# State-space part of a two-block kernel: the decay matrices as single-pass products in two parts, and the closing norm multiplication moved into the attention

## The reference, cut to what matters

```python
a_cum = jnp.cumsum(A, -1)
Lmat = jnp.exp(segsum(A))            # exp(a_cum[l] - a_cum[s]) where s <= l, else 0
y_diag = einsum('bclhn,bcshn,bhcls,bcshp->bclhp', Cc, Bc, Lmat, X)
chunk_states = einsum('bclhn,bhcl,bclhp->bchpn', Bc, exp(a_cum[..., -1:] - a_cum), X)
# carried over the chunks:  state = state * exp(a_cum[..., -1]) + chunk_states
y_off = einsum('bclhn,bchpn,bhcl->bclhp', Cc, prev, exp(a_cum))
y = (y_diag + y_off + d_skip * xs) * silu(z)
y = y * rsqrt(mean(y**2, -1) + eps) * norm_w
```

## Time and profile before

| what | us |
|---|---|
| median of 3 runs (lowest, highest) | 3704.17 (3702.64, 3704.63) |
| span of the profiled execution, first to last instruction | 3696.6 |
| difference of the two (what lies around the span) | 7.6 |
| first stage of the state space, first to last instruction | 308.7 to 319.7 |
| in it, end of VectorE's last instruction / of ScalarE's last | 318.6 / 319.7 |
| in it, end of VectorE's small chain (`adt`) / start of the product that needs it | 315.1 / 316.8 |
| in it, VectorE's first three instructions, together | 308.75 to 309.5 |
| second stage of the state space | 320.0 to 398.8 |
| in it, one square of ScalarE with its accumulator read | 0.9 |
| first products of the sparse attention | 399.1 |
| small tables issued with the key choice / first wait for them | 71.7 to 75.3 / 101.5 |

### The profile page before, as it was taken

How to read it: one execution, slowest core, us unless ns; L and a number is a source line. 1 busy time by engine, 2 the same in 40 slices (tenths; PEclk the granted TensorE clock), 3 DMA queues, 4 the chain that set the end, 5 groups by cost and what they waited for, 6 DMA issues and landing times. The chain is left out here.

```text
span 3696.6 us, 53818 instructions
## 1 busy us (share of the span) xinstructions
PE 3395.2 (92%) x18624; PEld 2593.7 (70%) x18624; DVE 2611.2 (71%) x4213; ACT 2064.5 (56%) x3299; POOL 374.7 (10%) x300
## 2 busy tenths in 40 slices
PE   8999989699969998998699999899989995999996
PEld 5444668577748764877588888788648784888885
DVE  3996755688762376663899999632766638999996
ACT  2663551488731475552477777523755524777674
POOL 0012000122121002000011111010020000111110
PEclk9999899799989999999899999999999997999998
DMA  3000011767261101013699999611010136999997
GB/s 147 23 1 3 2 69 70 295 257 270 100 230 42 46 10 44 2 60 141 233 396 379 384 390 379 253 43 46 2 52 1 54 117 240 388 380 394 380 381 285
DMA packets 115346, 645.96 MB, mean 175 GB/s; under 512 B 14048, under 2 KB 17120, under 8 KB 62944
## 3 DMA queue, kind: packets, MB, share of 16 engines
q1 hardware_dynamic: 94720, 569.15, 39.3%
q0 software_dynamic: 15984, 58.20, 5.3%
q10 hardware_dynamic: 4464, 16.25, 1.1%
HBM read 581.17 MB, written 62.39 MB: 174 GB/s over the span
## 5 line engine op out<-in xcount | busy, mean ns | idle before, releaser
L3375 DVE TENSOR_TENSOR low_ring<-mix,high_ring 128x2048 fp32r<-128x2048 f32 x256 | 576.7, 2284 | 41.4 <-ACT high_ring L3324 41.4
L3324 ACT ACTIVATE high_ring<-mix 128x2048 fp32r<-128x2048 f32 x256 | 477.0, 1931 | 80.3 <-PEq L141 80.3
L3263 PE MATMUL ps<-high_ring,x_high 128*128 128x512 f32 x1024 | 409.0, 399 | 8.5 <-DVE low_ring L3375 5.5
L3265 PE MATMUL ps<-high_ring,x_low 128*128 128x512 f32 x1024 | 399.6, 390 | 0.0
L3264 PE MATMUL ps<-low_ring,x_high 128*128 128x512 f32 x1024 | 399.2, 390 | 0.0
L3375 DVE TENSOR_TENSOR low_ring<-more_raw,high_ring 128x2048 fp32r<-128x2048 f32 x128 | 290.1, 2286 | 24.6 <-ACT high_ring L3324 24.6
L3324 ACT ACTIVATE high_ring<-more_raw 128x2048 fp32r<-128x2048 f32 x128 | 246.3, 1924 | 0.0
L3263 PEld LDWEIGHTS ps<-high_ring,x_high 128*128 128x128 f32 x1024 | 192.2, 188 | 71.3 <-DVE low_ring L3375 18.3
L3265 PEld LDWEIGHTS ps<-high_ring,x_low 128*128 128x128 f32 x1024 | 192.2, 188 | 41.6
L3264 PEld LDWEIGHTS ps<-low_ring,x_high 128*128 128x128 f32 x1024 | 192.5, 188 | 37.4
L3263 PE MATMUL ps<-high_ring,h_high 128*128 128x512 f32 x512 | 205.5, 401 | 0.0
(11 more groups left out here) (506 smaller groups left out, 8091.1 us busy)
## 6 DMA issues: line engine op xcount, KB each, us to landing
mix<-in_expert_units SPq DMA_DIRECT2D x256, 1024.0 KB, 7.6
more_raw<-in_expert_units SPq DMA_DIRECT2D x128, 1024.0 KB, 8.6
raw_experts<-in_expert_units SPq DMA_DIRECT2D x16, 3072.0 KB, 11.5
expert_out<-out ACTq DMA_DIRECT2D x31, 512.0 KB, 2.6
qk_body<-residual SPq DMA_DIRECT2D x16, 512.0 KB, 7.0
mix<-in_w_turned SPq DMA_DIRECT2D x16, 512.0 KB, 4.1
qk_tail<-in_w_out SPq DMA_DIRECT2D x8, 1024.0 KB, 8.2
mix<-residual SPq DMA_DIRECT2D x16, 512.0 KB, 3.3
```

Source lines behind the costliest of these rows:

```text
L3263: nc.tensor.matmul(ps[:, bank, :], left_high, high, start=first, stop=False)
L3265: return nc.tensor.matmul(ps[:, bank, :], left_low, high, start=False, stop=final)
L3324: nc.scalar.activation(w_high[:, n % RING, :], raw[n % RAW_UNITS], ACT.Copy).then_inc(high_ready, 1)
L3375: nc.vector.tensor_tensor(w_low[:, n % RING, :], raw[n % RAW_UNITS], w_high[:, n % RING, :].bitcast(F32), ALU.subtract).then_inc(low_ready, 1)
```

## The change

Spans. The running sums inside a chunk are now also made transposed, in one product in the first stage: `adt` (128 x 64) turned by `upto` gives 64 rows, one per chunk and head, of 128 running sums. VectorE splits them into a rounded part and a remainder (`cum_high`, `cum_low`). GpSimd makes rounded (fp32r) copies of the identity, of `hidden` (for 4 heads) and of a selector of chunks, `chunk_r` (64 x 8 x 128). At the start of the second stage VectorE and GpSimd each multiply one part with the selector of heads: `sums_high` and `sums_low` (64 x 1024 each). From then on the spans of a chunk are, per bank, three single-pass fp32r products: identity x hidden, chunk selector x sums_high, chunk selector x sums_low. `a_upto` and VectorE's product per chunk are gone. `hidden` is loaded as one 128 x 128 tile, with a new table `places`, among the small tables of `choose_keys`; the 256 KB load in the first state-space stage is gone.

Norm. The eight products with `root` and `norm_w` leave the state space and stand on VectorE in the attention, one in each of its iterations p = 4 to 11. The reciprocal stays.

```diff
@@ attend_pairs: VectorE, loop over p
                 copy_groups(p)
+                if gated and 4 <= p < 4 + T:
+                    rows, root, weight = gated
+                    nc.vector.scalar_tensor_tensor(out=rows[:, p - 4, :], in0=rows[:, p - 4, :],
+                                                   scalar=root[:, p - 4:p - 3], in1=weight, op0=ALU.mult,
+                                                   op1=ALU.mult)
                 if p >= 3:
                     write(p - 3)
@@ state_space, first stage
+                pe.wait_ge(read, 12)
+                nc.tensor.matmul(ps[0:TH, 5, 0:P], adt[:, :, :].rearrange("p t h -> p (t h)"), upto[:, :],
+                                 start=True, stop=True, skip_group_check=True).then_inc(turned_full, 1)
+            @block.gpsimd
+            def _(pool):
+                nc.gpsimd.tensor_copy(ident_r[:, :], ident[:, :])
+                nc.gpsimd.tensor_copy(hidden_r[:, :, :], hidden[:, :].unsqueeze(1).broadcast_to([P, 4, P]))
+                nc.gpsimd.tensor_copy(chunk_r[:, :, :], spread(places[0:TH, H:H + T], [TH, T, P]))
...
+                dve.wait_ge(turned_full, 1)
+                chain.step(nc.vector.tensor_copy(cum_high[:, :], ps[0:TH, 5, 0:P]))
+                nc.vector.tensor_tensor(cum_low[:, :], ps[0:TH, 5, 0:P], cum_high[:, :].bitcast(F32),
+                                        ALU.subtract)
@@ state_space, second stage, TensorE
                 def span(c):
-                    pe.wait_ge(a_upto_ready, c + 1)
-
+                    if c == 0:
+                        pe.wait_ge(sums_ready, 2)
+
+                    if c >= 1:
+                        pe.wait_ge(spans_ready, c)
                     for h in range(2):
-                        nc.tensor.matmul(ps[:, h, :], ident[:, :], hidden[:, :, :].rearrange("p a b -> p (a b)"),
+                        four = slice(4 * h, 4 * h + 4)
+                        nc.tensor.matmul(ps[:, h, :], ident_r[:, :], hidden_r[:, :, :].rearrange("p a b -> p (a b)"),
                                          start=True, stop=False)
-                        last = nc.tensor.matmul(ps[:, h, :], ones[:, :],
-                                                a_upto[:, 4 * h:4 * h + 4, :].rearrange("p a b -> p (a b)"),
+                        nc.tensor.matmul(ps[:, h, :], chunk_r[:, c, :],
+                                         sums_high[:, four, :].rearrange("p a b -> p (a b)"), start=False, stop=False)
+                        last = nc.tensor.matmul(ps[:, h, :], chunk_r[:, c, :],
+                                                sums_low[:, four, :].rearrange("p a b -> p (a b)"),
                                                 start=False, stop=True)
...
+                inside(0)
                 span(0)
-                inside(0)
                 span(1)
@@ second stage, GpSimd, ahead of its loop
+                nc.gpsimd.tensor_tensor(sums_low[:, :, :], cum_low[:, :].unsqueeze(1).broadcast_to([TH, H, P]),
+                                        spread(places[0:TH, 0:H], [TH, H, P]), ALU.mult).then_inc(sums_ready, 1)
@@ second stage, VectorE
-                steps_upto(0)
-                steps_upto(1)
+                nc.vector.tensor_tensor(sums_high[:, :, :],
+                                        cum_high[:, :].bitcast(F32).unsqueeze(1).broadcast_to([TH, H, P]),
+                                        spread(places[0:TH, 0:H], [TH, H, P]), ALU.mult).then_inc(sums_ready, 1)
                 pairs_of(0)
                 for c in range(T):
-                    if c + 2 < T:
-                        steps_upto(c + 2)
                     if c + 1 < T:
                         pairs_of(c + 1)
...
-                chain.step(nc.vector.reciprocal(root[:, :], root[:, :]))
-                for c in range(T):
-                    nc.vector.scalar_tensor_tensor(out=ssd[:, c, :], in0=ssd[:, c, :], scalar=root[:, c:c + 1],
-                                                   in1=norm_w[:, :], op0=ALU.mult, op1=ALU.mult)
+                nc.vector.reciprocal(root[:, :], root[:, :])
```

More of the change, by code:

```diff
@@ L273, in halves, with attend_pairs @@
     return ap.rearrange("p (a b) -> p a b", a=2)
-def attend_pairs(book, ps, ident, pairs, scale, widest, tables=None):
+def attend_pairs(book, ps, ident, pairs, scale, widest, tables=None, gated=None):
     nc = book.nc
@@ L1111, in state_space @@
     nc = book.nc
-    upto, bias, a_log, skip, norm_w = consts
+    upto, bias, a_log, skip, hidden, places, root = consts
     H = SSD_HEADS
+    TH = T * H
     G = H // 2
@@ L1117, in state_space @@
         xs = sb("xs", [P, T, 5 * P])
-        hidden = sb("hidden", [P, 4, P])
         dt = sb("dt", [P, T, H])
@@ L1129, in state_space @@
         ss = sb("ss_ssd", [P, T])
[L1130 to L1135, removed]
+        rounded = lambda name, shape: ctx.enter_context(nc.sbuf_tensor(name, shape, F32R))
+        ident_r = rounded("ident_r", [P, P])
+        hidden_r = rounded("hidden_r", [P, 4, P])
+        chunk_r = rounded("chunk_r", [TH, T, P])
+        cum_high = rounded("cum_high", [TH, P])
+        cum_low = sb("cum_low", [TH, P])
+        with Stage(book, "full", "read", "exp_a", "exp_x", "one_more", "logged", "adt_ready", "cum_full", "turned_full",
+                   "cum_read", "fades", "dve_steps") as (
+                block, full, read, exp_a, exp_x, one_more, logged, adt_ready, cum_full, turned_full, cum_read,
+                fades, steps):
             raw_dt = small[:, :, DT0:DT0 + H]
@@ L1206, in _ @@
                 nc.vector.tensor_tensor(u1[:, :, :], u2[:, :, :], cum[:, :, :], ALU.subtract).then_inc(cum_read, 1)
-        with Stage(book, "a_upto_ready", "spans_full", "spans_ready", "pairs_full", "pairs_ready", "x_ready",
+                dve.wait_ge(turned_full, 1)
+                chain.step(nc.vector.tensor_copy(cum_high[:, :], ps[0:TH, 5, 0:P]))
+                nc.vector.tensor_tensor(cum_low[:, :], ps[0:TH, 5, 0:P], cum_high[:, :].bitcast(F32),
+                                        ALU.subtract)
+        with Stage(book, "sums_ready", "spans_full", "spans_ready", "pairs_full", "pairs_ready", "x_ready",
                    "inner_full", "outer_full", "state_full", "state_ready", "decayed", "skip_ready", "y_ready",
                    "gated", "squares", "means", "roots", "pool_steps", "dve_steps") as (
-                block, a_upto_ready, spans_full, spans_ready, pairs_full, pairs_ready, x_ready, inner_full,
+                block, sums_ready, spans_full, spans_ready, pairs_full, pairs_ready, x_ready, inner_full,
                 outer_full, state_full, state_ready, decayed, skip_ready, y_ready, gated, squares, means, roots,
@@ L1215, in state_space @@
             sb = lambda name, shape: inner.enter_context(nc.sbuf_tensor(name, shape, F32))
-            a_upto = sb("a_upto", [P, H, P])
+            sums_high = inner.enter_context(nc.sbuf_tensor("sums_high", [TH, H, P], F32R))
+            sums_low = inner.enter_context(nc.sbuf_tensor("sums_low", [TH, H, P], F32R))
             spans = sb("spans", [P, H, P])
@@ L1341, in _ @@
                 chain = Chain(dve, steps)
[L1343 to L1347, removed]
                 def pairs_of(c):
@@ L3502, in block_one @@
             masks = sb(choice, "masks", [P, moff[T - 1] + S])
+            norm_w = sb(choice, "norm_w", [P, BANK])
+            root = sb(choice, "root_ssd", [P, T])
             with ExitStack() as early:
@@ L3513, in block_one @@
                 skip = sb(early, "skip", [P, SSD_HEADS])
-                norm_w = sb(early, "norm_w", [P, BANK])
+                hidden = sb(early, "hidden", [P, P])
+                places = sb(early, "places", [P, SSD_HEADS + T])
                 with ExitStack() as projection:
@@ L3522, in block_one @@
                                  (skip[:, :], A["d_skip"].broadcast_to([P, SSD_HEADS])),
+                                 (hidden[:, :], A["hidden"]), (places[:, :], A["places"]),
                                  (norm_w[:, :], A["ssd_norm_w"].broadcast_to([P, BANK]))])
                 state_space(book, ps, A, ident, ones, xbc[:, :, 0:S], small, z, ssd,
-                            (upto, dt_bias, a_log, skip, norm_w))
-            attend_pairs(book, ps, ident, sparse_pairs(raw, small, masks, moff, heads_out), HD ** -0.5, S)
+                            (upto, dt_bias, a_log, skip, hidden, places, root))
+            attend_pairs(book, ps, ident, sparse_pairs(raw, small, masks, moff, heads_out), HD ** -0.5, S,
+                         gated=(ssd, root, norm_w[:, :]))
         rows = heads_out
@@ L3746, in constants @@
     hidden = np.where(np.arange(P)[:, None] <= np.arange(P)[None, :], f(0), f(HIDE)).astype(f)
-    out["hidden"] = np.ascontiguousarray(np.broadcast_to(hidden[:, None, :], (P, 4, P)))
+    out["hidden"] = hidden
+    row = np.arange(P)[:, None]
+    out["places"] = np.concatenate([row % SSD_HEADS == np.arange(SSD_HEADS), row // SSD_HEADS == np.arange(T)],
```

(1 more changed line is left out.)

2 lines of the change are left out of this document (removed).

## The result

The changed kernel takes 3716.51 us (median of 20 runs, 3708.2 to 3731.4), the kernel before in the same comparison 3703.24 (20 runs): ratio 1.0031, 95% interval 1.0023 to 1.0039. It is slower by some 0.3%; the forecast was 3694.6 and faster.

A forecast was written before the change was run, and what follows sets the result against it. It took TensorE and VectorE both to be full in the second state-space stage, behind ScalarE's exponentials every 7.06 us. Terms 2.9 - 4.5 - 7.3 + 0.4 - 2.2 + 1.1 = -9.6 gave 3694.6 us, range 3686 to 3702.

The forecast's parts named there:

- Five turns: Second state-space stage, chunks 2 to 7: turns of 5.6 us, bound by VectorE, 28.0 for 35.3, so -7.3 us.
- Rival B: Second-stage loop: pauses drop TensorE to the low clock, turns cost it 7.9 us, 3706.2, slower than before; chance 0.11.
- Rival C: First-stage casts or second-stage 64-row products are dear, turns of 8.6 us, 3714 and more; chance 0.05.
- rival A: End of second stage: clock stays up, transposes and last inner faster, 4.1 us more gain, 3690.5; chance 0.17.
- Start, -4.5: Second stage's start to chunk 2's exponential: it comes at 337.7 instead of 342.16, -4.5 us.
- Casts, +2.9: First stage: three GpSimd casts hold up VectorE's third instruction, exponential at 313.1 instead of 310.12, +2.9 us.
- rule of blocking: First-stage casts: GpSimd and VectorE instructions wait for the whole of each other's; with it +2.9 us, without it 0.
- without slack: First stage: from the exponential at 310.12 ScalarE runs without slack to the stage's end, so its delay counts.
- -2.2 at the stage's end: Second stage's end: norm products of 5.39 us go, but the stage then waits for the transposes, so only -2.2 us.
- +1.1 in the attention: Attention: eight norm products of 0.67 us on VectorE, mostly covered by its idle time, +1.1 us; bounds 0 and +5.4.
- Last chunk, +0.4: Second stage, last chunk's exponential to the transposes: 10.6 us instead of 10.2, +0.4 us.

The follow-up runs named there:

- run 2: The changed kernel with its sums and chunk selector written over 128 rows, the selector's upper 64 zero: 3687.33 us, ratio 0.9946 to the kernel before.
- run 5: The changed kernel with high and low parts of the sums in one 128-row operand, one product per half instead of two: 3689.59 us, ratio 0.9959 to before.
- run 10: The kernel of run 5 with 36 instead of 60 transposes at the stage's end: 3683.75 us, ratio 0.9953 to the kernel before.
- run 9: The kernel of run 2 with the norm products back in the state space: 3690.50 us, ratio 0.9976 to the kernel before.
- run 6: The kernel of run 2 with only the low part of the sums and its selector back at 64 rows: 3716.20 us, ratio 1.0031 to before.
- run 8: The changed kernel with 12 filler transposes ahead of each chunk's span products from chunk 1 on: 3704.24 us, ratio 0.9995 to the kernel before.

## Why the prediction was wrong

**Five turns, the step that failed.** It took "VectorE is the bound" and the granted clock 1.00 from before's loop. At 1.00 the term was right: 5.59 for 5.6 forecast, with VectorE at 9.64 of 10 and `state_new` stretched to 1.04 us as forecast (run 2). But the level did not come along: four of the six span products use half of the 128 rows, the number of rows changes three times among the six, and the loop stays at 0.50, with turns of 9.79 that TensorE bounds. Before's loop could not show that: its span and inner products all have 128 rows, and it is at 1.00 although inside and outer have 64.

**Rival B** named the low clock and the sign, but with a wrong reason and too low a price. It feared the pauses of a faster loop; run 2 has them (8.98 of 10 busy) at 1.00, and the changed kernel has next to none (68.69 of 70) at 0.50. The Trainium skill, page "TensorE: Matmul & The Clock Gate", section "What's actually happening", ties the level to how busy TensorE has been lately; between these two loops the busy time that the trace lists does not decide it. Against B the prediction held that "dense work brought the level up in this stage": true of before's products, not of these. Its turn was 7.9: six entries at 0.46 make 2.76, measured 3.60; the rest 2.4, measured 2.76; inner 2.8, measured 3.43., from which the entry came, are products that all have 128 rows.

**Rival C** gives the measured time, "3714 and more", but by luck: it wants entries of 0.86 us and turns of 8.6 at the full clock, and they are 0.42 to 0.72 at half of it, in turns of 9.79. The sum of **rival A** is off by a little: 8.95 - 6.0 + 1.0 is 3.95, not 4.1.

**Start, -4.5.** The sums came as forecast: the first span began at 323.06 for 323.6. The gain was lost behind it: the exponentials of chunks 0, 1 and 2 come at 326.92, 333.00 and 341.64, for 326.5, 331.5 and 337.7 forecast. The clock stays at 0.50, and six span products there take 3.6 us, not 2.7. With 1.00 by 328 the gain is 10.3 us, counted from the stage's start (11.92 in run 5, 22.18 before); run 5 also has two products fewer per chunk and earlier sums.

**Casts, +2.9.** The rule of blocking held, the price did not. First stage, GpSimd's casts and VectorE's three instructions (0.2 us each before, with the exponential at 310.12):

```profile
308.86 0.29 POOL L1171 CAST ident_r<-ident 128x128 fp32r<-128x128 f32 x1 [41.31 <-POOLq L141]
308.89 0.34 DVE L1199 TENSOR_TENSOR dt<-small,dt_bias 128x64 f32<-128x64 f32 x1 [4.86 <-remote]
...
309.10 0.61 POOL L1172 CAST hidden_r<-hidden 128x512 fp32r<-128x512 f32 x1
309.26 0.49 DVE L1200 TENSOR_SCALAR u<-dt 128x64 f32<-128x64 f32 x1
309.65 1.04 POOL L1173 CAST chunk_r<-places 64x1024 fp32r<-64x1024 f32 x1
309.79 0.97 DVE L1201 TENSOR_TENSOR u<-u,dt 128x64 f32<-128x64 f32 x1
...
310.80 0.26 ACT L1180 ACTIVATE u<-u 128x64 f32<-128x64 f32 x1 [0.45 <-DVE u L1201]
```

VectorE's third ends with the third cast. But the casts take 1.94 us together, not 3.8 (1.2 ns an element, not 2.3), so ScalarE's exponential is at 310.80, not 313.1. Of the 0.7 left against before, 0.1 reaches the stage's end, so ScalarE did not run "without slack" either: before, it stood still 0.30 us ahead of its last copies (317.07), and `adt` was ready 1.7 us before the product that needs it.

**Norm.** The -2.2 at the stage's end was right (-2.4). The +1.1 in the attention was not: 122.64 us with the eight products there, 126.68 before. What the forecast did not price is the clock at the attention's start, 0.50 for 13.6 us before and 1.00 now. The products' own cost is not shown apart from it. With the products and 0, 6.8 and 10.2 us at 0.50 the attention takes 122.64, 125.39 and 126.63 (the changed kernel, runs 5 and 10), some 0.4 a us; if that holds up to 13.6 us, it would take 128.0 there, and before, without the products, took 126.68. So the products would cost 1.3, an estimate from these runs, and the clock would give 5.3.

**Last chunk, +0.4.** +3.0: 13.2 us at 0.50, where run 2, at 1.00 for most of it, takes 11.0. The forecast's own terms add up to 10.8, not 10.6.

## What to carry to other kernels

A faster form of a product is priced at the level that it lets TensorE have, not at the level that the old form had: look at how many of the 128 rows each new product uses before taking over a granted clock. Fill the rows (here the two parts of a split operand side by side, which also saves two of six products) and put products of equal rows next to each other. Where the work behind a barrier starts with TensorE, price the pause in front of it: behind a pause of 2.60 us instead of 0.30 the attention took 4.0 us longer, 1.2 of them made good in the stage after it (runs 9 and 2).

## What the runs showed of the hardware that was not expected

- A stream of products, busy 68.69 of 70 us, at a granted clock of 0.50 throughout; the same products with zero rows added, 1.00 from 341 to 374.
- A weight load that does not run beside the product before it where the number of rows changes: entries beside a change 0.56 to 0.73 us instead of 0.42 at 0.50 (run 6), 0.32 to 0.43 instead of 0.23 at 1.00 (run 8).
- The moment at which the level rises differs between executions of one kernel (fp32 at 64 rows: near 380, or not before 440, past the loop; filler: near 333 or 344).
- What stays open: by what quantity rows and their order hold the level down, and why the clock fell some 4 and 3 us into the attention in runs 5 and 10, behind pauses of 0.30 and 0.80 us, and not in run 2 behind 0.30.
